# Attention scores of two heads: 128-row products of high and low parts, or 64-row products side by side

## The chip, the core and the metric

The kernel runs on one core of one Trainium2 chip, as one launch. The metric is the device time of a run in microseconds (us). The kernel before takes 1893.79 us, the median of three runs (1891.71 to 1893.83). The profile was taken on one further execution, of 1892.18 us, whose profiled span is 1890.4 us.

The engines are named as in the profile: PE is the matrix engine, PEld its weight loads, DVE the vector engine, ACT the scalar engine, POOL the general one, SP the one that issues most DMAs. PE writes its products to PSUM, which has eight banks of 128 partitions by 512 fp32 numbers.

## The reference

The program is one inference step of a two-layer decoder: a retention layer, a projection to shared keys and values, and a stick-breaking attention layer with 16 heads of 64 numbers each. A prompt of 1024 tokens and eight sample groups of eight tokens use the same weights. The change touches only the attention, where this is computed for each head of the prompt:

```
z = q @ k.T * scale + bias            # (1024 queries x 1024 keys), 64 numbers in each product
mask = k_pos < q_pos                  # strictly causal
log_keep = where(mask, log_sigmoid(-z), 0)
tail_excl = sum of log_keep over the later keys of the same query
w = where(mask, exp(log_sigmoid(z) + tail_excl), 0)
o = w @ v
```

The queries and keys are normed before, and the output is multiplied by a gate.

## The kernel before, in words

**The work.** The function `attention` handles the 16 heads in eight pairs. A pair has eight units, one for each block of 128 queries; unit t needs the (t + 1) * 128 keys up to its own. A unit is cut into pieces. A piece with up to 256 keys holds both heads of the pair next to each other (a joint piece); a wider one, 384 or 512 keys, holds one head, so its two heads are two pieces. Units with more than 512 keys have two such spans. That makes 20 pieces per pair, 160 in all, and with 8 pieces for the samples 168 (`NPC`). Odd pairs go through their units from wide to narrow, even ones from narrow to wide.

**Stages of a piece.** `score` (PE, L1715) writes the scores of a piece to one of the two banks of `z`. `stick` (ACT, L1910) reads them twice, for sigmoid(-z), called `keep`, and sigmoid(z), called `take`. `weigh` (DVE, L2033) makes the running product of `keep` (a scan, L2052) and multiplies it into `take` (L2062). `turn_w` (PE, L1750) transposes the result into one of the two banks of `wt`, ACT (or for a few pieces DVE) copies it to `w_t`, and `attend` (PE, L1761) multiplies the values by it into `out`, which has two banks, one for each group of four units. DVE's `gate` (L2111) empties a bank of `out`.

**Order.** Every engine runs a loop over p, and the order is written out in these loops. In step p PE does `score(p + 1)`, a turn of keys, queries or sample pages if one is due, `turn_w(p - 2)` and `attend(p - 3)`; `attend` has work only where a piece closes a unit's span, that is, for a joint piece or the second head. Between these, in the first part of the section, PE does the projection of the gates (`project`, lines L2934 to L2936, L2956 and L2957), cut into slices that are dealt out over the steps by `slices_before`. ACT does `stick(p)`, the copy of the weights of p - 2 and the copies of what was turned; DVE does `weigh(p - 1)` and the rest. `score(p + 1)` waits until `take` of piece p - 1 is made (L1718), which frees the bank of `z`.

**Precision.** Queries and keys are fp32. A 4-byte operand in the reduced format fp32r goes through PE once, so the kernel works with two parts. A key row is split into a high part (rounded to fp32r, by ACT, L1898) and the rest (DVE, L2025); the two are laid side by side in `k_parts`, 64 + 64 numbers, and turned, so that `k_t` has the high part of the 64 numbers on partitions 0 to 63 and the low part on 64 to 127. The queries of a head are loaded twice side by side (`load_q`, four DMAs, L1326), turned, and the turned 128-row block is kept as `q_hi` (ACT, L1908) and the rest `q_lo` (DVE, L2030). A head's scores are then two accumulated fp32r products of 128 rows each, L1741 with `q_hi` and L1745 with `q_lo`. A joint piece adds the bias by a product (L1744), and the span with the own block adds the mask by a product (L1747). All that is turned for queries, keys and samples goes through one bank, `kq`, and each turn waits until the one before has been copied out (`kq_taken`). Queries are turned in 32 groups of two units (`QG = 2`, four transposes each), keys in four turns of four transposes per pair.

## Time and profile before

| what | value |
|---|---|
| median of the runs | 1893.79 us |
| the profiled execution | 1892.18 us |
| its span | 1890.4 us |
| PE busy | 1808.4 us, 96% |
| DVE busy | 1054.8 us, 56% |
| ACT busy | 810.1 us, 43% |
| PE, DVE, ACT busy from 1366 to 1560 us | 179.53, 156.91, 140.42 us |
| PE, DVE, ACT busy from 1560 to 1781 us | 200.79, 191.27, 179.63 us |

The attention section runs from the first score at 1366.2 us to the last `attend` at 1781 us. The gate projection is dealt out in its first half, the samples in its second. Busy times of PE include the modelled end of each product, so that successive products overlap in time; what a product costs in a stream is the distance from its start to the next start. PE runs at 2.4 GHz for almost the whole program.

One fp32 product (not fp32r) leaves two MATMUL records and two weight loads in the trace.

### The profile page before, as it was taken

What the parts mean: (1) busy time and instruction counts of PE and PEld (TensorE: products, weight loads), DVE (VectorE), ACT (ScalarE), POOL (GpSimd) and SP (SyncE); (2) the same over time, 40 slices, a digit from 0 to 9 for tenths busy, and PEclk for the clock granted to TensorE, in tenths of its full rate; (3) what the DMA queues carried; (4) which work ended last, traced back from release to release, by engine and by line L of the source; (5) the groups of instructions that cost most, each with busy time, mean ns of one, the idle gap of its engine ahead of it and who ended that gap; (6) DMA issues with size and microseconds to landing.
All of it is one profiled execution on the core that took longest, in us unless ns stands there. A gap on an engine that the chain in (4) does not pass through costs nothing. (4 is left out here: it accounts for less than half of the span.)

```text
span 1890.4 us, 28031 instructions
## 1 busy us (share of the span) xinstructions
PE 1808.4 (96%) x10103; PEld 1427.4 (76%) x10103; DVE 1054.8 (56%) x1975; ACT 810.1 (43%) x1682; POOL 81.0 (4%) x140
## 2 busy tenths in 40 slices
PE   5899999999999999999999999999989988999998
PEld 2678787878787878677788777888777766676677
DVE  4553535353535353624546345755178788888852
ACT  3742323232323333412344223533367677878620
POOL 2000000000000000000000000011000000000000
PEclk8899999999999999999999999999999999999999
DMA  9231212131303040583424563223323253553152
GB/s 324 84 93 58 93 57 92 57 99 50 125 23 126 22 148 0 194 272 96 133 62 173 203 214 111 82 92 113 110 59 84 79 164 102 157 154 127 57 178 95
DMA packets 184939, 215.54 MB, mean 114 GB/s; under 512 B 45352, under 2 KB 142560, under 8 KB 183809
## 3 DMA queue, kind: packets, MB, share of 16 engines
q1 hardware_dynamic: 171146, 167.17, 28.9%
q0 software_dynamic: 13696, 47.08, 6.5%
q8 instruction: 60, 0.98, 0.2%
q14 instruction: 37, 0.30, 0.1%
HBM read 165.39 MB, written 48.83 MB: 113 GB/s over the span
## 5 line engine op out<-in xcount | busy, mean ns | idle before, releaser
L475 PE MATMUL rt_acc<-rt_w_hi,rt_h_hi 128*128 128x512 f32 x504 | 203.5, 404 | 1.0 <-DVE rt_h_lo L1014 1.0
L477 PE MATMUL rt_acc<-rt_w_hi,rt_h_lo 128*128 128x512 f32 x504 | 197.4, 392 | 0.0
L476 PE MATMUL rt_acc<-rt_w_lo,rt_h_hi 128*128 128x512 f32 x504 | 196.7, 390 | 0.0
L1057 DVE TENSOR_TENSOR rt_by_cos<-rt_raw,rt_cos 128x256 f32<-128x256 f32 (+1 forms) x72 | 30.5, 424 | 243.9 <-ACT rt_raw L887 243.9
L898 ACT COPY rt_qk_t<-rt_tr 128x256 f32<-128x256 f32 (+1 forms) x72 | 26.0, 361 | 278.6 <-PE rt_tr L706 278.6
L2946 PE MATMUL kq_acc<-kq_w_hi,kq_h 128*128 128x512 f32 x320 | 127.3, 398 | 0.0
L2949 PE MATMUL kq_acc<-kq_w_hi,kq_h 128*128 128x512 f32 x320 | 124.8, 390 | 0.0
L2947 PE MATMUL kq_acc<-kq_w_lo,kq_h 128*128 128x512 f32 x320 | 124.8, 390 | 0.0
L1938 ACT COPY pa_w_t<-pa_wt 128x512 f32<-128x512 f32 (+2 forms) x160 | 86.7, 542 | 72.2 <-PE pa_wt L1756 69.1
L477 PEld LDWEIGHTS rt_acc<-rt_w_hi,rt_h_lo 128*128 128x128 f32 x504 | 94.6, 188 | 20.5
L475 PEld LDWEIGHTS rt_acc<-rt_w_hi,rt_h_hi 128*128 128x128 f32 x504 | 94.9, 188 | 19.1 <-DVE rt_h_lo L1014 1.4
L2052 DVE TENSOR_TENSOR_SCAN pa_after_key<-pa_keep 128x128 f32<-128x128 f32 (+3 forms) x128 | 101.6, 814 | 12.9 <-ACT pa_keep L1919 6.1
L476 PEld LDWEIGHTS rt_acc<-rt_w_lo,rt_h_hi 128*128 128x128 f32 x504 | 95.0, 189 | 17.9 <-issue 0.2
L764 PE MATMUL rt_acc_g<-rt_h_hi,rt_g_hi 128*128 128x512 f32 x256 | 105.8, 413 | 0.0
L2062 DVE TENSOR_TENSOR pa_take<-pa_take,pa_after_key 128x512 f32<-128x512 f32 (+2 forms) x160 | 102.1, 638 | 5.5
L766 PE MATMUL rt_acc_g<-rt_h_lo,rt_g_hi 128*128 128x512 f32 x256 | 100.3, 392 | 0.0
L765 PE MATMUL rt_acc_g<-rt_h_hi,rt_g_lo 128*128 128x512 f32 x256 | 100.1, 391 | 0.0
L1756 PE MATMUL pa_wt<-ident,pa_take 128*128 128x128 f32 x592 | 94.0, 276 | 3.9 <-DVE pa_take L2062 2.2
L1741 PE MATMUL z<-pa_k_t,pa_q_hi 128*128 128x128 f32 (+3 forms) x192 | 79.7, 415 | 17.4 <-DVE pa_q_lo L2030 8.0
L1927 ACT ACTIVATE pa_keep<-z,pa_bias 128x512 f32<-128x512 f32 (+1 forms) x128 | 86.2, 673 | 16.4 <-PE z L1747 7.2
L2052 DVE TENSOR_TENSOR_SCAN pa_after_key<-pa_keep,pa_after_key 128x512 f32<-128x512 f32 x64 | 82.0, 1281 | 6.7 <-ACT pa_keep L1927 2.3
L1928 ACT ACTIVATE pa_take<-z,pa_bias 128x512 f32<-128x512 f32 (+1 forms) x128 | 85.7, 669 | 0.0
(414 smaller groups left out, 4168.7 us busy)
## 6 DMA issues: line engine op xcount, KB each, us to landing
ro_a_raw<-retained SPq DMA_DIRECT2D x14, 1024.0 KB, 5.8
op_ada<-in_ada_w SPq DMA_DIRECT2D x8, 1024.0 KB, 11.4
rt_w_raw<-in_ret_w_in SPq DMA_DIRECT2D x16, 512.0 KB, 5.1
rt_w_raw<-in_ret_w_in SPq DMA_DIRECT2D x8, 1024.0 KB, 7.8
rt_old<-in_state_ret SPq DMA_DIRECT2D x8, 1024.0 KB, 6.0
rt_g_raw<-in_ret_w_in SPq DMA_DIRECT2D x8, 1024.0 KB, 5.2
out_st_sample<-rt_new POOLq DMA_DIRECT2D x8, 1024.0 KB, 8.0
kq_w_raw<-in_sb_w_in SPq DMA_DIRECT2D x4, 2048.0 KB, 9.0
```

Source lines behind the costliest of these rows:

```text
L475: nc.tensor.matmul(dst, h_hi[:, k, cols], w_hi[:, k, :], start=k == 0, stop=False)
L476: nc.tensor.matmul(dst, h_hi[:, k, cols], w_lo[:, k, :], start=False, stop=False)
L477: last = nc.tensor.matmul(dst, h_lo[:, k, cols], w_hi[:, k, :], start=False, stop=k == KD - 1)
L764: nc.tensor.matmul(dst, g_hi[:, k, part], h_hi[:, k, cols], start=k == 0, stop=False)
L765: nc.tensor.matmul(dst, g_lo[:, k, part], h_hi[:, k, cols], start=False, stop=False)
L766: last = nc.tensor.matmul(dst, g_hi[:, k, part], h_lo[:, k, cols], start=False, stop=k == KD - 1)
L1756: last = nc.tensor.transpose(wt[:, p % 2, b * P:(b + 1) * P], take[:, p % TR, b * P:(b + 1) * P], ps.ident[:])
L2052: nc.vector.tensor_tensor_scan(ring[:, c0:c0 + n][:, ::-1], k[:, ::-1], k[:, ::-1], seed, ALU.mult, ALU.bypass).then_inc(scanned, 1)
L2062: nc.vector.tensor_tensor(own, own, later, ALU.mult).then_inc(weighed, 1)
L2946: nc.tensor.matmul(dst, hi, w_hi, start=k == 0, stop=False)
L2947: last = nc.tensor.matmul(dst, hi, w_lo, start=False, stop=t == NPT and k == KD - 1)
L2949: last = nc.tensor.matmul(dst, proj.lo(t)[:, k, :], w_hi, start=False, stop=k == KD - 1)
```

## The change

- `k_parts`, the splits of keys and of queries and their semaphores are gone, on ACT and DVE, in the attention and at the end of the projection before it. `k2` gets two buffers.
- Keys and queries are kept in fp32 as they are turned: 128 numbers of a row are the two heads of a pair, so a turned block has head 0 on partitions 0 to 63 and head 1 on 64 to 127. A pair now has two turns of keys instead of four; queries are turned in 16 groups of four units (`QG = 4`), with one DMA for what were four.
- The scores of two heads are computed together, in a round: two fp32 products of 64 rows, one at row position 0 and one at row position 64, each to a bank of its own. There are two pairs of banks (`z2`), used in turn by rounds. The bias and mask products stay, 128 rows each. A round is two pieces where a piece holds one head, else one. `score` of the next round is issued at the first piece of a round.
- Two banks (`wt`) take all that is turned, weights, keys, queries, new rows and pages, in one alternating sequence, and each turn waits until the turn two before it has been copied out (`wait_bank`). `kq` is gone, and `out` has one bank.
- On DVE the gate of p - 4 is moved ahead of `weigh(p - 1)`.

```diff
@@ attention @@
-        QG = 2
+        QG = 4
+        rounds = []
+        for p in range(NPC):
+            if pieces[p].heads == (1,):
+                rounds[-1].append(p)
+            else:
+                rounds.append([p])
+        round_of = {p: r for r, members in enumerate(rounds) for p in members}
...
-        z, wt, acc, kq, out = held.z, bank("wt", 2), bank("acc"), bank("kq"), bank("out", 2)
+        z2, wt, acc, out = (held.z, bank("z2", 2)), bank("wt", 2), bank("acc"), bank("out")
...
+        turns = [("k", 0, 0), ("q", 0), ("k", 0, 1)]
+        for p in range(NPC):
+            if p in q_slots:
+                turns.append(("q", q_slots[p]))
+            if p in k_slots:
+                turns.append(("k", *k_slots[p]))
...
+            if p >= 2:
+                turns.append(("w", p - 2))
...
+        def wait_bank(engine, *turn):
+
+            n = turn_of[turn] - 2
...
+            if kind == "k":
+                engine.wait_ge(k_taken, 2 * key[0] + key[1] + 1)
+            elif kind == "q":
+                engine.wait_ge(q_taken, key[0] + 1)
...
+            else:
+                wait_taken(engine, key[0])
...
@@ PE @@
-            def score(p):
-                at = pieces[p]
-                if p >= 2:
-                    pe.wait_ge(sticks, p - 1)
+            def score(r):
+                p = rounds[r][0]
+                at, z = pieces[p], scores_of(p)
+                if r >= 2:
+                    pe.wait_ge(sticks, rounds[r - 2][-1] + 1)
...
-                for i, hh in enumerate(at.heads):
-                    dst, keys = z[:, p % 2, i * n:(i + 1) * n], k_t[:, pair % 2, hh, c0:c0 + n]
-                    nc.tensor.matmul(dst, q_hi[:, g % 2, hh, at.u % QG, :], keys, start=True, stop=False)
-                    if len(at.heads) == 2:
+                own, joined = c0 + n == (t + 1) * P, len(at.heads) == 2
+                for hh in range(2):
+                    part = slice(hh * DH, (hh + 1) * DH)
+                    last = nc.tensor.matmul(z[:, hh, 0:n], q_t[part, g % 2, at.u % QG, :], k_t[part, pair % 2, c0:c0 + n],
+                                            start=True, stop=not (own or joined), tile_position=(hh * DH, 0))
...
-            turn_k(0, 0)
-            project(0, 2)
-            turn_k(1, 0)
-            project(2, 4)
+            project(0, 3)
             turn_q(0)
...
             for p in range(NPC):
-                if p + 1 < NPC:
-                    score(p + 1)
+                if p == rounds[round_of[p]][0] and round_of[p] + 1 < len(rounds):
+                    score(round_of[p] + 1)
...
@@ DVE @@
-            rest_q(0)
...
             for p in range(NPC):
+                if p >= 4:
+                    gate_at(p - 4)
                 if p:
                     weigh(p - 1)
                 if p >= 2:
                     take_w(p - 2)
-                if p - 1 in q_slots:
-                    rest_q(q_slots[p - 1])
-                if p >= 4:
-                    gate_at(p - 4)
```

How the change moves instructions shows at three places. The first is PE near the end of the section, in the last pair, where two units of 512-key spans and a narrow one follow each other. Before, `z<-pa_k_t,pa_q_hi` and `z<-pa_k_t,pa_q_lo` are the two products of one head's scores, `pa_wt<-ident` turns weights, `pa_kq<-ident` turns queries:

```order
L1741 MATMUL z<-pa_k_t,pa_q_hi 128x512
L1745 MATMUL z<-pa_k_t,pa_q_lo 128x512
L1747 MATMUL z<-pa_far_r_3481,pa_ident_r_3482 128x128
L1756 MATMUL pa_wt<-ident,pa_take 128x128 x2
L1805 MATMUL pa_acc<-sa_v_pages_8036,pa_w_t 32x256 x8
L1805 MATMUL pa_acc<-sa_new_rows_8035,pa_w_t 32x256 x4
L1741 MATMUL z<-pa_k_t,pa_q_hi 128x512
L1745 MATMUL z<-pa_k_t,pa_q_lo 128x512
L1747 MATMUL z<-pa_far_r_3481,pa_ident_r_3482 128x128
L1676 MATMUL pa_kq<-ident,pa_q4_3487 128x128 x4
L1756 MATMUL pa_wt<-ident,pa_take 128x128 x4
```

The same place of the changed kernel; `pa_q_t` are the turned queries, and "x2" at a score are the products of the two heads:

```order
L1771 MATMUL z<-pa_k_t,pa_q_t 128x512 x2
L1779 MATMUL z<-pa_far_r_3481,pa_ident_r_3482 128x128 x2
L1788 MATMUL pa_wt<-ident,pa_take 128x128 x2
L1790 MATMUL pa_wt<-ident,pa_take 64x128
L1816 MATMUL pa_out<-pa_w_t,pa_v2 64x128 x8
L1788 MATMUL pa_wt<-ident,pa_take 128x128 x2
L1837 MATMUL pa_acc<-sa_v_pages_8024,pa_w_t 32x256 x8
L1837 MATMUL pa_acc<-sa_new_rows_8023,pa_w_t 32x256 x4
L1771 MATMUL pa_z2<-pa_k_t,pa_q_t 128x384 x2
```

The scores of both heads stand together, the next step begins without any, and the turn of queries at this place is gone. The second place is DVE at the start of the section, before; `pa_after_key<-pa_keep` is the scan, `pa_q_lo` the rest of the queries, `pa_k_parts` that of the keys:

```order
L2030 TENSOR_TENSOR pa_q_lo<-pa_kq,pa_q_hi 128x512
L2140 TENSOR_TENSOR pa_g_out_3478<-pa_acc,pa_g_out_3478 128x512
L2052 SCALAR_TENSOR_TENSOR pa_after_key<-pa_keep 128x128 x2
L2062 TENSOR_TENSOR pa_take<-pa_take,pa_after_key 128x256
L2030 TENSOR_TENSOR pa_q_lo<-pa_kq,pa_q_hi 128x512
L2052 SCALAR_TENSOR_TENSOR pa_after_key<-pa_keep 128x256 x2
L2062 TENSOR_TENSOR pa_take<-pa_take,pa_after_key 128x512
L2052 SCALAR_TENSOR_TENSOR pa_after_key<-pa_keep 128x384
L2062 TENSOR_TENSOR pa_take<-pa_take,pa_after_key 128x384
L2030 TENSOR_TENSOR pa_q_lo<-pa_kq,pa_q_hi 128x512
```

The same place of the changed kernel:

```order
L2148 TENSOR_TENSOR pa_g_out_3478<-pa_acc,pa_g_out_3478 128x512
L2060 SCALAR_TENSOR_TENSOR pa_after_key<-pa_keep 128x128 x2
L2070 TENSOR_TENSOR pa_take<-pa_take,pa_after_key 128x256
L2060 SCALAR_TENSOR_TENSOR pa_after_key<-pa_keep 128x256 x2
L2070 TENSOR_TENSOR pa_take<-pa_take,pa_after_key 128x512
L2060 SCALAR_TENSOR_TENSOR pa_after_key<-pa_keep 128x384
```

The three `pa_q_lo` instructions are gone, and scans and multiplications follow each other without them. The third place is PE a little earlier, from the second score of the program on; first before:

```order
L1688 MATMUL pa_kq<-ident,pa_k_parts_3477 128x128 x4
L1741 MATMUL z<-pa_k_t,pa_q_hi 128x256
L1744 MATMUL z<-pa_bias_parts_3485,pa_share_3486 128x256
L1745 MATMUL z<-pa_k_t,pa_q_lo 128x256
L1747 MATMUL z<-pa_far_r_3481,pa_ident_r_3482 128x128
L1741 MATMUL z<-pa_k_t,pa_q_hi 128x256
L1744 MATMUL z<-pa_bias_parts_3485,pa_share_3486 128x256
L1745 MATMUL z<-pa_k_t,pa_q_lo 128x256
L1747 MATMUL z<-pa_far_r_3481,pa_ident_r_3482 128x128
L1676 MATMUL pa_kq<-ident,pa_q4_3487 128x128 x4
```

And in the changed kernel:

```order
L1771 MATMUL pa_z2<-pa_k_t,pa_q_t 128x256 x2
L1776 MATMUL pa_z2<-pa_bias_parts_3485,pa_share_3486 128x256
L1779 MATMUL pa_z2<-pa_far_r_3481,pa_ident_r_3482 128x128
L1776 MATMUL pa_z2<-pa_bias_parts_3485,pa_share_3486 128x256
L1779 MATMUL pa_z2<-pa_far_r_3481,pa_ident_r_3482 128x128
L1708 MATMUL pa_wt<-ident,pa_q4_3487 128x128 x4
L1771 MATMUL z<-pa_k_t,pa_q_t 128x384 x2
```

The turn of keys ahead of this score is gone, and the score of the third unit (384 keys) uses queries that were turned with the first two.

## Rows read from the trace of the kernel before

**Rows 1.** Busy us of each engine in the attention's two halves.

```profile
1366.00:1560.00 194.00, 179.53 (x1363) 141.95 (x1361) 156.91 (x207) 140.42 (x265) 8.52 (x13) 0.98 0.36 101
1560.00:1781.00 221.00, 200.79 (x1899) 152.09 (x1897) 191.27 (x280) 179.63 (x362) 2.14 (x4) 1.00 0.43 127
```

**Rows 2.** DVE and ACT groups by form, 1366 to 1781 us: count, busy, mean ns, idle before.

```profile
L2052 DVE TENSOR_TENSOR_SCAN pa_after_key<-pa_keep,pa_after_key 128x512 f32<-128x512 f32 x64 | 82.0, 1281 | 6.7 <-ACT pa_keep L1927 2.3 <-DVE pa_g_t L2118 0.6
L2062 DVE TENSOR_TENSOR pa_take<-pa_take,pa_after_key 128x512 f32<-128x512 f32 x112 | 77.5, 692 | 3.9
L2030 DVE TENSOR_TENSOR pa_q_lo<-pa_kq,pa_q_hi 128x512 fp32r<-128x512 f32 x31 | 21.3, 686 | 7.0 <-ACT pa_q_hi L1908 7.0
L2025 DVE TENSOR_TENSOR pa_k_parts<-pa_k,pa_k_parts 128x512 fp32r<-128x512 f32 x14 | 9.6, 687 | 0.7
L1908 ACT CAST pa_q_hi<-pa_kq 128x512 fp32r<-128x512 f32 x31 | 18.4, 594 | 0.8 <-PE pa_kq L1676 0.8
```

**Rows 3.** Waits of PE, 1366 to 1781 us: total us, times, longest.

```profile
PE z L1741 <- DVE pa_q_lo L2030: 8.0, 5, 3.9
PE pa_kq L1688 <- ACT pa_k_t L1902: 3.1, 9, 0.8
```

**Rows 4.** Timeline of PE, 1764 to 1769 us: start, length, line, tiles, shapes.

```profile
1766.74 0.50 PE L1741 MATMUL z<-pa_k_t,pa_q_hi 128*128 128x512 f32 x1
1767.08 0.40 PE L1745 MATMUL z<-pa_k_t,pa_q_lo 128*128 128x512 f32 x1
1767.32 0.22 PE L1747 MATMUL z<-pa_far_r,pa_ident_r 128*128 128x128 f32 x1
1767.38 0.60 PE L1676 MATMUL pa_kq<-ident,pa_q 128*128 128x128 f32 x4
1767.81 0.60 PE L1756 MATMUL pa_wt<-ident,pa_take 128*128 128x128 f32 x4
1768.34 0.44 PE L1784 MATMUL pa_out<-pa_w_t,pa_v 128*64 128x128 f32 x4
1768.71 0.44 PE L1741 MATMUL z<-pa_k_t,pa_q_hi 128*128 128x384 f32 x1
1768.99 0.34 PE L1745 MATMUL z<-pa_k_t,pa_q_lo 128*128 128x384 f32 x1
```

**Rows 5.** Timeline of PE, 1366 to 1379 us.

```profile
1368.92 0.36 PE L1741 MATMUL z<-pa_k_t,pa_q_hi 128*128 128x256 f32 x1
1369.12 0.27 PE L1744 MATMUL z<-pa_bias_parts,pa_share 128*128 128x256 f32 x1
1369.23 0.28 PE L1745 MATMUL z<-pa_k_t,pa_q_lo 128*128 128x256 f32 x1
1369.35 0.22 PE L1747 MATMUL z<-pa_far_r,pa_ident_r 128*128 128x128 f32 x1
...
1369.87 0.63 PE L1676 MATMUL pa_kq<-ident,pa_q 128*128 128x128 f32 x4
1374.38 0.66 PE L1741 MATMUL z<-pa_k_t,pa_q_hi 128*128 128x384 f32 x1 [3.88 <-DVE pa_q_lo L2030]
```

**Rows 6.** Timeline of PE in the retention layer, 127.4 to 128.8 us.

```profile
127.48 0.48 PE L745 MATMUL rt_acc<-rt_v,rt_k_own 32*128 32x256 f32 x1
...
127.50 0.48 PE L745 MATMUL rt_tr<-rt_v,rt_k_own 32*128 32x256 f32 x1
127.80 0.37 PE L745 MATMUL rt_acc<-rt_v,rt_k_own 32*128 32x256 f32 x1
...
128.02 0.38 PE L745 MATMUL rt_acc<-rt_v,rt_k_own 32*128 32x256 f32 x1
```

**Rows 7.** Timeline of PE, 1763 to 1800 us: fp32 products of 128 rows.

```profile
1781.41 6.28 PE L1880 MATMUL z<-ao_w_raw,ao_a_raw 128*128 128x512 f32 x14
```

**Rows 8.** Timeline of DVE, 1366 to 1379 us.

```profile
1371.84 0.69 DVE L2140 TENSOR_TENSOR pa_g_out<-pa_acc,pa_g_out 128x512 f32<-128x512 f32 x1 [6.10 <-ACT pa_g_out L1972]
...
1373.56 0.68 DVE L2030 TENSOR_TENSOR pa_q_lo<-pa_kq,pa_q_hi 128x512 fp32r<-128x512 f32 x1
```

More of the change, by code:

```diff
@@ L1322, in load_q @@
         rows_of = ps.q_rows[0:SEQ, :].rearrange("(t p) c -> p t c", p=P)
-        src = rows_of[:, 4 * half:4 * half + 4, pair * 2 * DH:(pair + 1) * 2 * DH].rearrange("p t (h d) -> p t h d", h=2)
-        for a in range(2):
-            for hh in range(2):
-                sp.dma_start(self.q4[:, m % 3, :, hh, a, :], src[:, :, hh, :]).then_inc(loaded, 16)
+        src = rows_of[:, 4 * half:4 * half + 4, pair * 2 * DH:(pair + 1) * 2 * DH]
+        sp.dma_start(self.q4[:, m % 3], src).then_inc(loaded, 16)
 class Held:
@@ L1518, in wait_taken, with turn_bank, scores_of @@
                 engine.wait_ge(w_taken_a, len([n for n in range(p + 1) if not on_vector(n)]))
+        turns = [("k", 0, 0), ("q", 0), ("k", 0, 1)]
[4 more added lines that the diff above has]
+                turns.append(("k", *k_slots[p]))
+            if p in new_slots:
+                turns.append(("new", new_slots[p]))
+            if p in page_slots:
+                turns.append(("pages", *page_slots[p]))
+            if p >= 2:
+                turns.append(("w", p - 2))
+        turns += [("w", NPC - 2), ("w", NPC - 1)]
+        turn_of = {turn: n for n, turn in enumerate(turns)}
+        def turn_bank(*turn):
+            return wt[:, turn_of[turn] % 2, :]
+        def wait_bank(engine, *turn):
+            n = turn_of[turn] - 2
+            if n < 0:
+                return
+            kind, key = turns[n][0], turns[n][1:]
+            if kind == "k":
+                engine.wait_ge(k_taken, 2 * key[0] + key[1] + 1)
+            elif kind == "q":
+                engine.wait_ge(q_taken, key[0] + 1)
+            elif kind == "new":
+                engine.wait_ge(*((new_taken, key[0] + 1) if key[0] < 2 else (sa_ready, 1)))
+            elif kind == "pages":
+                engine.wait_ge(sk_taken, 4 * key[0] + key[1] + 1)
+            else:
+                wait_taken(engine, key[0])
+        def scores_of(p):
+            return z2[round_of[p] % 2]
         def sample_before(p, lag):
@@ L1879, in _ @@
                 a = held.raw[:, 0, k, :] if k < held.LOADED else held.own_raw[:, t * P:(t + 1) * P]
-                nc.tensor.matmul(z[:, 0, :], a, first.raw[:, k, :], start=k == 0, stop=k == KD - 1).then_inc(first_made, 1)
+                nc.tensor.matmul(held.z[:, 0, :], a, first.raw[:, k, :], start=k == 0, stop=k == KD - 1).then_inc(first_made, 1)
             t += 1
@@ L1906, in take_q @@
                 if g >= 2:
[L1907 to L1908 removed]
+                    act.wait_ge(scored, round_of[ends[QG * (g - 1) - 1]] + 1)
+                nc.scalar.copy(q_t[:, g % 2].rearrange("p n c -> p (n c)"), turn_bank("q", g)).then_inc(q_taken, 1)
             def stick(p):
[L1911 to L1912 removed]
+                at, n, z = pieces[p], pieces[p].wide, scores_of(p)
+                act.wait_ge(scored, round_of[p] + 1)
                 if p >= 2:
@@ L2720, in _ @@
                     nc.scalar.copy(pairs.ident_r[:], ps.ident[:])
-                    act.wait_ge(k_loaded, 16)
-                    for hh in range(2):
-                        nc.scalar.copy(pairs.k_parts[:, hh, :, 0, :], by_head(pairs.k2, hh)).then_inc(k_hi_s, 1)
         @block.vector
```

196 lines of the change are left out of this document (77 added, 119 removed).

## The prediction

> **What bounds the kernel now.** I read the busy times by stage first. The change touches only the attention, 1366 to 1781 us. In its first half PE is busy 179.53 of 194 us and DVE 156.91; in the second PE 200.79 of 221, DVE 191.27, ACT 179.63 [rows 1]. So the first half, with the gate projection in it, is PE's. In the second PE and DVE are nearly level: where pieces of 512 keys follow each other, DVE needs 1281 + 692 ns, 1.97 us, for each, and splits of queries and keys on top [rows 2]; where there are narrow pieces and sample pages, PE has more to do. Next the waits: PE's longest single wait is one of 3.9 us for the low part of the queries, and all five waits of that kind are 8.0 us; waits for the one bank of turned keys come to 3.1 us, and sample turns add some more [rows 3]. Last the timelines, which give what a product costs from start to start.
>
> The whole section is one chain of three engines in step, so a microsecond saved counts only on the engine that is late there. I count by halves.
>
> **Turns.** Queries go from 32 groups to 16 of four transposes, keys from 32 turns to 16. That is 128 transposes less. Four take 1767.38 to 1767.81, 0.43 us [rows 4], so 0.108 us each, 13.8 us on PE, about half of it in each half of the section.
>
> **The score products.** Before, a head at 512 keys costs 0.34 + 0.24 = 0.58 us (1766.74, 1767.08, 1767.32), at 384 keys 0.28 us and then, between the 0.24 and the 0.12 of its neighbours, 0.18 us, together 0.46 [rows 4]. At 256 keys it is 0.20 + 0.12 us (the bias product between them stays) for the first head [rows 5], and about 0.29 for the second, which follows a product and not a turn; at 128 keys some 0.25 per head, since no product there starts less than 0.11 us after another. A pair has six rounds at 512 keys and two each at 384, 256 and 128: 6 x 1.16 + 2 x 0.92 + 2 x 0.61 + 2 x 0.50 = 11.0 us, times eight pairs 88 us.
>
> After, an fp32 product is two records. At 128 rows the trace has 14 records of 512 columns, each 0.59 us long, in 6.28 us, so (6.28 - 0.59) / 13 = 0.44 us from start to start [rows 7]; a product is 0.88 us. Two heads one after the other would be 1.76 us and lose against 1.16. It hangs on whether products at different rows of the array run at the same time. The retention layer has the case, with four strips of 32 rows in four banks: four records start between 127.48 and 127.50, the next four from 127.80, the next from 128.02, each 256 columns wide [rows 6]. They run together, at 0.22 us for 256 columns, the price of one, and the first step to the second record is 0.10 us longer. I take the same for two strips of 64 rows. A round is then 0.43 + 0.43 + 0.10 = 0.96 us at 512, 0.74 at 384, 0.53 at 256, 0.31 at 128 (columns in proportion). Per pair: 6 x 0.96 + 2 x 0.74 + 2 x 0.53 + 2 x 0.31 = 8.9 us, times eight 71 us. That is 17 us less.
>
> Against it: PE must change over between full products and strips. The last of four turns of weights starts at 1767.81 + 0.60 - 0.28 = 1768.13, would end its turn at 1768.24, and the first `attend` product, in strips of 64 columns, starts at 1768.34 [rows 4]: 0.10 us. Each of the 96 prompt rounds is now followed by full products, a change-over that was not there. Ahead of a score one is new only where no `attend` stands before it: counted in the order, 43 of the rounds. 139 times 0.10 is 13.9 us. So the scores give 17 - 14 = 3 us; bounds: 17 with free change-overs, -11 if one costs 0.20.
>
> The Trainium skill ("TensorEngine Tiling (Array Packing)", Key Properties) speaks against the change here: "Changing tiling mode (not just tile) drains the TensorE". It names no price; by it every change-over counts, and the 0.10 us of the row bears it out. Without it the sum would be 14 us lower.
>
> **Start of the section.** PE sits idle 3.88 us until 1374.38 because the score of unit 2 needs the low part of its queries, and that DVE instruction (1373.56) stands behind a gate product, which itself waited 6.10 us, and the first `weigh` [rows 5, 8]. Now unit 2's queries were turned with the first two units', the score is done in that gap, and PE goes on when the first weights are ready, about 1373.6. I count 1.5 us, and 0.5 for less time at the lower clock after it: 2 us.
>
> **What leaves DVE and ACT.** DVE loses 31 query splits at 0.686 and 14 key splits at 0.687 us, 31 us [rows 2]; half of it, 15.5 us, in the second half. ACT loses 16 query copies at 0.594 us [rows 2], as many key copies and 14 key splits, some 28 us. In the first half PE hides all of it: nothing. In the second, where DVE is late it counts fully, where PE is late it does not. Bounds 0 and 15.5. PE's own saving there is 7 us of turns, and the four later waits for query parts go, 8.0 - 3.9 = 4.1 us [rows 3]. So the half is shorter by 11 us where PE is late and by 15.5 where DVE is; I take 11 in all, since nothing says which.
>
> **What the change adds in waits.** (1) A piece's weights now share two banks with keys, queries and pages. After such a turn in step p, `turn_w` of step p + 1 waits for ACT's copy of it; `attend` and the next scores stand behind it on PE, and ACT's copy of the weights behind these. There are 15 query, 14 key, 3 new-row and 32 page turns, 64. The copy is 0.59 us and stands behind ACT's `stick` and weight copy, while PE has a score (0.96) or an `attend` in between. Bounds 0 and 0.6 us each, 0 to 38 us; nearest row: the nine waits of key turns for ACT's copy in the old single bank, 3.1 us together, 0.35 each [rows 3]. PE had slack in part of these: I take 0.05 each, 3 us, net of the old waits that go. (2) `out` has one bank: 15 times `attend` waits for DVE's gate, one 0.69 us product like the one in rows 8, while PE turns weights for 0.43 us. 0.1 us each, 1.5 us; bounds 0 and 0.7 each, 10. (3) Scores come in lumps: a step with 0.96 us of scores, then one with none. ACT's copy waits up to 0.4 us in the first, PE in the second; the scores are ready a step earlier, so ACT no longer waits for them. I call it even; bounds -4 and +8.
>
> The DMAs for queries become one of 512-byte rows instead of four; nothing waits for them in the rows, so 0. The splits before the section run beside PE's projection: 0.
>
> **Sum.** First half: turns -7, scores -1.5, start -2, new waits +1.5: -9. Second half: -11 with its turns, scores -1.5, new waits +3: -9.5. Together -18.5, in round figures -19, against the execution of 1892.18 us: 1873. The median of the runs stands 1.6 us above that execution; that is less than this sum can tell, so it stays at 1873.
>
> **Rivals.** (A) Deeper gain: DVE was what held PE up in all of the second half, its 15.5 us come in full, and PE's idle time, 14.5 and 20.2 us in the two halves [rows 1], shrinks by 5 us. For it: DVE's 191 us is as high as PE's real load, since PE's busy time includes modelled ends. Against it: ACT waits for turned weights, so PE is late often. Then -15.5 - 9 - 5 = -30: 1862. (B) Little gain: change-overs to strips of rows cost 0.15 us and not 0.10 (+7), and narrow pieces and sample pages hold PE so that of the second half's 11 us only the 5 us that follow wide pieces come (+6): -19 + 7 + 6 = -6, 1886. For it: PE's load there is the highest of the three [rows 1]; against it: the first record's extra 0.10 us is counted already [rows 6]. (C) Slower: the shared turn banks. If the wait behind each of the 64 turns is over 0.33 us, the gain is gone; at the 0.6 us of a whole copy it is 38 us against the 3 counted, 1873 + 35 = 1908; at 0.45 us, which I take for it, 1873 + 26 = 1899. For it: PE and ACT are then in lock-step, and a `turn_w` held up holds the score of the next round. Against it: PE has 0.43 to 1.5 us of other work between, and ACT runs ahead on `stick`. (D) The strips do not run together, and the change does not do what it says. For it nothing in the rows, only that 64-row strips and this pairing don't occur. Then 48 x 0.86 + 16 x (0.64 + 0.43 + 0.21) = 62 us more: 1936.
>
> **Chances.** Forecast 0.47 (1867 to 1882), A 0.25, B 0.12, C 0.12, D 0.04. A difference under 0.2%, 3.8 us, can't be told from none. Faster than 1890: forecast, A and most of B, 0.82; within: 0.05 from B and the edge of C; slower 0.13. The range: A down to 1855 and B in full, 1892; C and D and the deepest of A are left out.
>
> **What would show it.** In the profile after: the score records of two heads start within 0.02 us of each other and the next two 0.53 us later at 512 columns (strips run together); the first mask product starts about 0.10 us after their end (change-over); 64 + 64 transposes of queries and keys at 0.108 us; no wait of 3.9 us at the start; DVE's busy time in the section lower by 31 us; waits of `turn_w` for ACT's copies of keys, queries or pages under 5 us in total. Score starts 0.43 us apart one by one would make it wrong at once (D), and large waits of turned weights for ACT copies would (C).

## The result, and the profile after

The changed kernel takes 1899.14 us (median, 1896.48 to 1901.40), the kernel before 1891.89 us (1890.73 to 1893.83, now six runs) on the same chip. The ratio is 1.0041, 95% interval 1.0030 to 1.0051: some 8 us slower, where 1873 and 19 us less were forecast. Of the rivals, C had named 1899, but for a reason that explains only part of it, as will be seen.

Busy time of each engine in the two halves, as in [rows 1] (the second half now goes on past 1781 us; the product behind the last `attend` starts at 1787.4):

```profile
1366.00:1560.00 194.00, 178.51 (x1290) 116.90 (x1289) 145.28 (x185) 126.90 (x239) 8.52 (x13) 0.99 0.27 86
1560.00:1781.00 221.00, 200.40 (x1791) 130.54 (x1792) 174.87 (x250) 167.26 (x333) 2.15 (x4) 0.98 0.38 120
```

PE's busy times are those of [rows 1] to about 1 us, while DVE has 28 us less to do and ACT 26. The work did leave DVE and ACT; the section got longer all the same. The groups by form (1366 to 1788 us) that answer to [rows 2]:

```profile
L2060 DVE TENSOR_TENSOR_SCAN pa_after_key<-pa_keep,pa_after_key 128x512 f32<-128x512 f32 x64 | 82.0, 1281 | 12.7 <-ACT pa_keep L1949 8.4 <-DVE pa_g_t L2126 0.9
L2070 DVE TENSOR_TENSOR pa_take<-pa_take,pa_after_key 128x512 f32<-128x512 f32 x112 | 77.5, 692 | 3.9
L2126 DVE TENSOR_TENSOR pa_g_t<-pa_out,pa_g_t 128x512 f32<-128x512 f32 x14 | 9.7, 691 | 21.7 <-PE pa_out L1816 21.7
L1929 ACT COPY pa_q_t<-pa_wt 128x512 f32<-128x512 f32 x15 | 8.9, 590 | 2.1 <-PE pa_wt L1708 2.1
```

The scan and the weighing cost what they did. Queries are now 15 copies on ACT and nothing on DVE. New is DVE's idle time of 21.7 us ahead of the gate product. Next the waits from 1366 to 1790 us, as in [rows 3]:

```profile
DVE pa_g_t L2126 <- PE pa_out L1816: 21.7, 13, 2.4
PEld pa_wt L1788 <- DVE pa_take L2070: 21.4, 26, 1.6
...
DVE pa_after_key L2060 <- ACT pa_keep L1949: 16.8, 23, 1.6
...
PE pa_wt L1788 <- DVE pa_take L2070: 8.9, 13, 1.3
...
PE pa_wt L1741 <- ACT sa_k_t L1983: 5.8, 6, 1.3
```

The waits for the low part of the queries (8.0 us) are gone. In their place DVE waits for PE's sums at the gate, and PE waits for DVE's weights before it turns them. A circle of two engines that wait for each other has no idle engine to relieve.

A round of two heads at 512 keys and what follows it, against [rows 4] (timeline of PE, 1766 to 1769.2 us):

```profile
1766.98 0.65 PE L1788 MATMUL pa_wt<-ident,pa_take 128*128 128x128 f32 x4
1767.56 1.13 PE L1771 MATMUL z<-pa_k_t,pa_q_t 64*128 64x512 f32 x4
1768.62 0.44 PE L1779 MATMUL z<-pa_far_r,pa_ident_r 128*128 128x128 f32 x2
1768.90 0.41 PE L1788 MATMUL pa_wt<-ident,pa_take 128*128 128x128 f32 x2
```

And the same view from 1767.8 to 1768.3 us, which cuts the group of four and shows only the two later records:

```profile
1768.10 0.60 PE L1771 MATMUL z<-pa_k_t,pa_q_t 64*128 64x512 f32 x2
```

Both heads' second records stand in one row of 0.60 us, the length of one record: the strips run together, 0.54 us behind the first two. Four transposes between two groups of strips take 0.58 us (1766.98 to 1767.56), where four among full products take 0.43 [rows 4]: 0.09 more from the last transpose to the first strip, and 0.05 more from the first transpose, which stands behind strips, to the second. From the second records to the first mask product it is 0.52 us, 0.43 for the 512 columns and 0.09 for the change back. Then comes what I had not counted: two mask products take 0.28 us (1768.62 to 1768.90), and a mask product alone 0.06 in [rows 4]. Without strips ahead the same two take 0.17 us (second experiment below). So the first product after the change back holds up the second by another 0.10 us; the other 0.05 us beyond twice 0.06 comes with the new order, in which two masks stand one behind the other.

The start, against [rows 5]:

```profile
1371.69 1.13 PE L1771 MATMUL pa_z<-pa_k_t,pa_q_t 64*128 64x512 f32 x4 [1.02 <-ACT pa_take L1942]
...
1374.76 0.66 PE L1788 MATMUL pa_wt<-ident,pa_take 128*128 128x128 f32 x4 [1.32 <-DVE pa_take L2070]
```

The stall of 3.88 us is gone, and two of 1.02 and 1.32 us stand in its place: 1.5 us less, as forecast. DVE's first gate product comes at 1370.80 after 10.46 us of waiting, against 1371.84 and 6.10 us in [rows 8]; no query split stands behind it:

```profile
1370.80 0.69 DVE L2148 TENSOR_TENSOR pa_g_out<-pa_acc,pa_g_out 128x512 f32<-128x512 f32 x1 [10.46 <-ACT pa_g_out L1996]
1371.41 0.73 DVE L2060 TENSOR_TENSOR_SCAN pa_after_key<-pa_keep 128x128 f32<-128x128 f32 x2
```

**PE's section added up.** I gave each PE record of the section the time to the next record's start, and split off idle time (a wait) and the 0.10 us at each change between full products and strips. The section here begins with the first turn of keys (1360.1 us before, 1358.1 after) and ends with the product behind the last `attend` (1781.4 and 1787.4), so it takes in some projection ahead of the first score. In us:

| | before | after | change |
|---|---|---|---|
| score products | 82.7 | 72.0 | -10.7 |
| turns of queries and keys | 28.4 | 15.2 | -13.2 |
| changes between full and strips (218, 369) | 21.8 | 37.9 | +16.1 |
| mask, bias, weight turns (they stand behind the changes) | 80.7 | 93.1 | +12.4 |
| all else | 162.4 | 163.6 | +1.2 |
| waits | 45.4 | 47.4 | +2.0 |
| section | 421.3 | 429.3 | +8 |

PE's own time was to fall by 17 us (turns 14, scores 3); it rose by 5.8. The 37.9 us are 1 us more than 369 times 0.10, so the +16.1 of the changes is 15 to 16. (The counts are those of the traces; a count of the order, in the expectation of the fifth experiment, gives 217 and 376.)

The rows of the changes and of what stands behind them grow by 28.5 us, 0.19 for each of 151 more changes. Not all of this is the price of a change. A second count, which takes a product's usual step from the trace itself and draws the line between work and wait a little otherwise, gives 79.0 us before and 92.4 after for masks, biases and weight turns, and 85.5 for the second experiment below, which has the new frame and no strips. So about half of the 12.4 us comes with the order of the new frame. What is left is 15 to 16 and some 7 us, 0.15 us for a change.

**The clock.** The two profiled executions differ in it as well. In this section PE's granted clock was at its lower level, 1.2 GHz, for 17.0 us after the change, in four stretches, of which these are two (stretch and length, busy us of PE, PEld, DVE, ACT and POOL, then the granted clock as a share of 2.4 GHz):

```profile
1358.50:1361.90 3.40, 3.40 (x11) 2.72 (x9) 1.78 (x1) 0.59 (x1) 0.00 (x0) 0.50 0.66 190
...
1559.90:1566.70 6.80, 6.69 (x34) 4.88 (x34) 5.27 (x12) 2.40 (x4) 0.00 (x0) 0.50 0.14 42
```

Before the change it was one stretch of 6.8 us:

```profile
1373.00:1379.80 6.80, 5.42 (x23) 4.76 (x23) 5.86 (x10) 3.21 (x7) 0.37 (x1) 0.50 0.40 93
```

They stand at or just behind idle time of PE: 2.39 us until 1358.10, 1.74 us until 1560.01, and before the change the 3.88 us of [rows 5]. In the first of them projection products start 0.43 us apart, behind it 0.23. PE was busy for 16.5 us of the four stretches and for 5.4 us of the one before; at half speed that costs at most 8.3 and 2.7 us. So up to 5.6 us of the 5.8 by which PE's own time rose in these two executions go with the clock. Over all runs it is less: the mean granted clock is 0.988 in the six runs of the changed kernel and 0.990 in the 78 runs of the kernel before that stand beside the experiments, and of these the ones at 0.988 took 1894.5 us and the ones at 0.991 1891.0, 1.2 us for 0.001. By that, an estimate, some 2 us of the 8 go with the clock. Whether more waits brought the lower clock or it came otherwise, no run tells.

### The profile page after: what moved, and what is told of

Its sections match the earlier page's. It is cut to its first block and busy times, and to the rows that moved or that the text cites. A ratio compares the mean times of both kernels' runs of the same rounds, so it can differ in the third digit from the quotient of the medians.

```text
span 1896.1 us, 27547 instructions
## 1 busy us (share of the span) xinstructions
PE 1812.8 (96%) x9975; PEld 1385.2 (73%) x9975; DVE 1029.3 (54%) x1927; ACT 787.7 (42%) x1634; POOL 81.2 (4%) x140
## 5 line engine op out<-in xcount | busy, mean ns | idle before, releaser
L1788 PEld LDWEIGHTS pa_wt<-ident,pa_take 128*128 128x128 f32 x592 | 67.2, 142 | 40.7 <-DVE pa_take L2070 21.4
L1816 PE MATMUL pa_out<-pa_w_t,pa_v 128*64 128x128 f32 x1152 | 85.5, 285 | 1.0 <-ACT pa_w_t L1961 0.7
L2382 DVE TENSOR_TENSOR ro_a_lo<-ro_a_raw,ro_a_hi 128x1024 fp32r<-128x1024 f32 x28 | 33.0, 1221 | 90.1 <-ACT ro_a_hi L2341 90.1
```

Of the source, the lines that this page charges most:

```text
L1788: last = nc.tensor.transpose(dst[:, b * P:(b + 1) * P], take[:, p % TR, b * P:(b + 1) * P], ps.ident[:])
```

## The experiments

Each was run beside the kernel before; ratios are against it, with 95% intervals. 0.1% is 1.9 us. The clock bears on some of them: the two with the longest waits have the lowest mean, 0.979 and 0.986. The expectations speak of three theories. Theory 1: PE's own time, above all the changes between full products and strips, ate the gain. Theory 2: the lumps of scores did. Theory 3: the frame did, that is the shared turn banks, the one output bank and the gate's place.

**Scores of the next round issued later** (changed kernel, one line):

```
-                if p == rounds[round_of[p]][0] and round_of[p] + 1 < len(rounds):
+                if p == rounds[round_of[p]][-1] and round_of[p] + 1 < len(rounds):
                     score(round_of[p] + 1)
```

> The changed kernel with one edit: the scores of the next round are issued at the last piece of a round, not at its first. In rounds of two pieces they then stand right behind an `attend`, so that 43 change-overs between full products and strips go, and the step that had no scores gets them. Theory 1 (PE's own time, above all 0.20 us for each change-over, 0.10 before the first strip or full product and 0.10 for the weights of the one behind it, has eaten the saving): 43 x 0.20 = 8.6 us less, 1890 to 1891. Theory 2 (the lumps of scores hold up the turns of weights, whose waits went from 4.7 to 19.1 us): the waits of turned weights fall back under 8 us as well, 1880 to 1885. Theory 3 (the shared turn banks cost the waits): the waits stay, 1890.

Measured 1888.74 us, 0.9982 (0.9973 to 0.9991): 0.59% less than the changed kernel. The waits of the section fall from 47.4 to 39.6 us, and its changes from 369 to 353, 16 and not the 43 expected. The place of the scores, which I had called even, costs some 10 us in this frame. By what mechanism is not shown: the waits of turned weights did not fall under 8 us, as theory 2 had it (21.4 before, 24.0 now for the wait of PEld on DVE's `take`), and the time lies between the two theories.

**Full products in place of strips** (changed kernel; each head's scores are two products of 128 rows in the rounded form, which add both heads up and use no low part):

```
-                    last = nc.tensor.matmul(z[:, hh, 0:n], q_t[part, g % 2, at.u % QG, :], k_t[part, pair % 2, c0:c0 + n],
-                                            start=True, stop=not (own or joined), tile_position=(hh * DH, 0))
+                    for time in range(2):
+                        last = nc.tensor.matmul(z[:, hh, 0:n], q_t[:, g % 2, at.u % QG, :], k_t[:, pair % 2, c0:c0 + n],
+                                                start=time == 0, stop=time == 1 and not (own or joined))
```

> The changed kernel without strips: each head's scores are two products of 128 rows in the reduced format on the turned block as it is, instead of one fp32 product of 64 rows. It leaves out that the two heads are kept apart (both heads get the sum over 128 rows) and the low parts. Rounds, banks, turns and waits are those of the changed kernel. Theory 1: some 150 change-overs at 0.20 us go, 30 us, and the products cost 83 us as in the kernel before and not 72, 11 us more: 19 us less than the changed kernel, 1880. Theories 2 and 3 (lumps or shared banks hold it): PE only waits longer, 1893 to 1899.

Measured 1886.09 us, 0.9971 (0.9962 to 0.9980), so the strips cost 0.70%, 13 us. PE's own time is 362.5 us against 381.8 in the changed kernel: of 19.3 us, 13 reach the end. That is between what theory 1 (1880) and the other two (1893 to 1899) expected. Two masks behind full products, to be set against 0.28 us behind strips:

```profile
1754.46 0.34 PE L1779 MATMUL z<-pa_far_r,pa_ident_r 128*128 128x128 f32 x2
1754.63 0.40 PE L1788 MATMUL pa_wt<-ident,pa_take 128*128 128x128 f32 x2
```

They take 0.17 us. 151 changes at 0.15 us are 23 us, the shorter score records give some 4 back, and 19 are left, as measured; some of it can be the clock, since PE was busy at the lower one for 6.7 us here and for 16.5 in the changed kernel.

**No splits on DVE** (kernel before; the queries' low parts are zero and the keys' are those of the first pair):

```
-                if p - 1 in q_slots:
-                    rest_q(q_slots[p - 1])
...
-                if p - 1 in k_split_slots:
-                    split_k(k_split_slots[p - 1])
```

> The kernel before with the splits of queries and keys taken from DVE: the low parts of the queries are zero, set once, those of the keys stay those of the first pair. PE and ACT do the same work. It measures the term of the prediction for DVE's relief alone. The prediction's reckoning: 11 us in the second half less the 4 us of waits that are counted in it, and the start, so 9 to 13 us less, 1879 to 1883. Theory 1 (PE's own time bounds both halves): only the waits for low parts, 8.0 us, go, and in part come back elsewhere: 3 to 6 us less, 1886 to 1889.

Measured 1883.72 us, 0.9961 (0.9948 to 0.9973): DVE's relief by itself is worth 8 us, all of it in PE's waits (45.4 to 36.4). It lies between the prediction's reckoning (9 to 13) and theory 1 (3 to 6).

**Half the turns** (kernel before; 118 transposes fewer, half of each turned block stale):

```
-                for hh in range(2):
+                for hh in range(2 if g < 1 else 1):
...
-                for n in range(4):
+                for n in range(4 if head < 2 else 2):
```

> The kernel before with half of the transposes in each turn of queries and keys after the first (118 transposes less); the other half of the turned block stays what was in the bank. ACT and DVE copy as much as before. It measures the prediction's term for turns alone. If PE bounds the section: 118 x 0.108 = 12.7 us less, 1879. If PE is late in only half of it: 6 us less, 1886. If ACT and DVE bound it: nothing, 1892.

Measured 1885.38 us, 0.9966 (0.9953 to 0.9979). The transposes cost what was forecast, 12.5 us of PE's own time; 6.5 reach the end, as if PE were late in half of the section, and PE's waits grow by 4.

**Strip work put together** (the version with late scores, and PE's last projection and fold of a step ahead of `attend`):

```
+                project(slices_before(p, 2), slices_before(p + 1, 0))
                 if p >= 3:
                     attend(p - 3)
-                project(slices_before(p, 2), slices_before(p + 1, 0))
```

> The changed kernel with the late scores of the experiment before, and in each step the last slices of the gate projection and the folds of the samples ahead of `attend`, so that `attend` and the scores of the next step stand together as strips. The order counts 376 change-overs in the changed kernel, 361 with late scores and 353 here (217 in the kernel before). Theory 1: 8 x 0.20 = 1.6 us less than with late scores, 1887. If `attend` is later than its copy for other reasons: up to 2 us more, 1889 to 1891.

Measured 1888.50 us, 0.9981 (0.9971 to 0.9990), the same as without. It saved 8 changes only, so it says nothing for or against theory 1.

**Shared turn banks alone** (kernel before; queries, keys and sample turns go to the weights' two banks):

```
-                pe.wait_ge(*kq_taken[0])
+                wait_bank(pe, "q", g)
...
-                        last = nc.tensor.transpose(kq[:, 0, at:at + P], src, ps.ident[:])
+                        last = nc.tensor.transpose(turn_bank("q", g)[:, at:at + P], src, ps.ident[:])
```

> The kernel before with the two turn banks shared by weights, keys, queries, new rows and pages, in one alternating sequence, as the changed kernel has them; the bank of its own for keys and queries is unused. Nothing else is changed. It measures the shared banks alone. Theory 3 (the shared banks cost the waits of turned weights, 4.7 to 19.1 us in the changed kernel): 8 to 14 us more, 1900 to 1906. Theories 1 and 2: -1 to +3 us, 1891 to 1895. The prediction counted 3 us for it.

Measured 1916.33 us, 1.0127 (1.0112 to 1.0142): 24 us more, where I had counted 3, and more than any theory expected. Its waits, 1366 to 1790 us, name the place:

```profile
PEld pa_wt L1786 <- DVE pa_take L2092: 26.1, 16, 3.2
PE pa_wt L1786 <- DVE pa_q_lo L2060: 24.4, 19, 3.0
```

The turn of weights waits, 19 times at 1.3 us, for the low part of the queries that lie in the bank, a split that DVE reaches a step later.

**The changed kernel's frame with the arithmetic of before** (rounds of scores, four score banks, shared turn banks, one output bank; high and low parts as before). Its core against the changed kernel:

```
-        k_t = sb("k_t", [P, 2, SEQ])
-        q_t = sb("q_t", [P, 2, QG, P])
+        k_t = sb("k_t", [P, 2, 2, SEQ], F32R)
+        q_hi = sb("q_hi", [P, 2, 2, QG, P], F32R)
+        q_lo = sb("q_lo", [P, 2, 2, QG, P], F32R)
```

> The changed kernel's frame with the arithmetic of the kernel before: scores of both heads in one lump at the first piece of a round, four score banks, shared turn banks, one bank of `out`, the gate ahead of `weigh`; but high and low parts, 128-row products, 32 groups of queries and 32 turns of keys as before, and all splits. It adds no change-overs. Theory 1 (the change-overs are the loss): the frame is free, 1890 to 1894. Theory 2 (lumps and the rest of the frame): 7 to 12 us more than before, 1899 to 1904.

Measured 1946.45 us, 1.0283 (1.0269 to 1.0296). With the old arithmetic the frame costs 54 us, where the dearest expectation was 12; the new arithmetic wins 46 of them back. The granted clock averages 0.979 here against 0.990, so by the 1.2 us above some 13 of the 54 go with it. Its waits from 1366 to 1790 us are those of the changed kernel, and the low part's besides:

```profile
PEld pa_wt L1800 <- DVE pa_take L2107: 36.0, 20, 4.0
PE pa_wt L1800 <- DVE pa_q_lo L2075: 33.5, 18, 3.7
DVE pa_g_t L2163 <- PE pa_out L1828: 28.4, 13, 4.2
```

**One output bank, and the gate ahead of `weigh`** (kernel before; the edits that make `out` one bank are left out below):

```
+                if p >= 4:
+                    gate_at(p - 4)
                 if p:
                     weigh(p - 1)
...
-                if p >= 4:
-                    gate_at(p - 4)
```

> The kernel before with one bank of `out` and the gate ahead of `weigh`, as in the changed kernel; nothing else. The prediction counted 1.5 us for the 15 waits. All theories: 0 to 3 us more, 1892 to 1895; if DVE's gate, now ahead of the scan of the next piece and waiting for `attend`, holds DVE up, 4 to 8 us more.

Measured 1898.42 us, 1.0035 (1.0022 to 1.0048). That is the case in which the gate holds DVE up (4 to 8 us more). The wait that it makes, from 1366 to 1790 us:

```profile
DVE pa_g_t L2118 <- PE pa_out L1784: 11.2, 12, 1.4
```

**The gate behind the weighing** (changed kernel; the edit is the last one turned round, between `weigh` and `take_w`):

```
-                if p >= 4:
-                    gate_at(p - 4)
                 if p:
                     weigh(p - 1)
+                if p >= 4:
+                    gate_at(p - 4)
```

> The kernel after the change (1899.1 us, 1.0041 of before) with one edit: VectorE gates the finished output of a group of four tiles behind the weighing of the same step and no longer ahead of it. It still has one output bank. Theory 3 (the frame of shared banks and waits costs the gain; in the kernel after, the gate waits 21.7 us for the sums of four steps ago, 13 times 2.4 us, and the scan and the weights queue behind it): the chain of scans keeps running, so 5 to 10 us less than after, 1889 to 1894, and 'gate waits for sums' falls under 8 us. Theory 1 (PE's own time of change-overs sets the end): PE's busy time is the same and so is the span, within 2 us of 1899. Against theory 3: with one output bank PE then waits for the gate before its next sums, 16 times up to 1.3 us, which could give most of it back.

Measured 1894.62 us, 1.0014 (1.0004 to 1.0024), 0.27% less than the changed kernel, at the edge of theory 3. The gate's wait for the sums (it was 21.7 us, 13 times up to 2.4 us, so 1.7 on average and not the 2.4 of the expectation) is down to 0.7 us, the scan waits longer for `keep` instead (16.8 to 27.7 us), and PE's wait before `attend` grows from 1.5 to 4.4 us, the price of the one bank itself (1.5 forecast).

**Urgent turn first** (changed kernel; queries, keys and pages are turned behind the weights):

```
                 project(slices_before(p, 0), slices_before(p, 1))
                 if p >= 2:
                     turn_w(p - 2)
+                if p in q_slots:
+                    turn_q(q_slots[p])
+                if p in k_slots:
+                    turn_k(*k_slots[p])
...
```

> The kernel after the change with one edit: in a step of PE the turn of queries, keys and sample pages comes behind the turn of the weights and no longer ahead of it, and the two shared turn banks are handed round in that order. Nothing is left out. Theory 3: the next turn of weights then waits for the copy of weights that the scalar engine makes first, and the turn after it for the copy of queries or keys, a step more of slack; the waits of the turn of weights fall from 19 us to 12 or less and the time by 4 to 8 us, to 1891 to 1895. Theory 1: same PE work, same time within 2 us of 1899.

Measured 1886.37 us, 0.9974 (0.9963 to 0.9985): 0.67%, 13 us less, more than expected. The waits that vanish are not those of the weights' turns (19.1 before, 22.8 now) but those of the turns moved: sample pages 8.7, keys 4.3 and queries 1.1 us become 0.4 together. My reason was wrong in its detail: what had stood in the way was the other turn's own wait for a bank, with the weights queued behind it.

**All three together**:

> The kernel after the change with three edits: the scores of the next round are issued at the last piece of the round and not at the first (alone 10.4 us less than after), the gate behind the weighing, and the turns of queries and keys behind the turn of weights. If the waits are separate stalls (theory 3), their gains add up and it takes 1875 to 1883, less than before's 1892 by 9 us or more. If PE's change-overs are a floor (theory 1: 382 us of products and change-overs in the section against 376 before), it stays near 1888.

Measured 1877.53 us, 0.9919 (0.9906 to 0.9932), faster than both kernels. The three gains were 0.59, 0.27 and 0.67%, in sum 1.53; together they bring 1.22. That is what separate stalls were expected to give (1875 to 1883), and not the floor of 1888. Its waits from 1366 to 1790 us:

```profile
ACT pa_w_t L1961 <- PE pa_wt L1788: 76.8, 80, 2.5
...
PEld pa_wt L1788 <- DVE pa_take L2070: 27.4, 34, 2.1
...
PE pa_wt L1788 <- DVE pa_take L2070: 10.4, 11, 2.0
```

What is left is the chain of a piece itself: DVE weighs, PE turns, ACT copies.

**All three, with full products in place of strips** (the edit of the second experiment on top):

> The kernel with all three reorderings (0.9919 of before, 1877.5 us), and in place of the two strips of 64 rows in full precision per pair of heads, two products of 128 rows in the rounded form for each head. What it computes changes: both heads are added into the same scores and no low part is multiplied in. It takes away about 140 change-overs between the two forms. Theory 1 (change-overs cost PE 0.20 us each): PE's products and change-overs in the section fall by 140 x 0.10 of change-over and some 3 us of products, and since the waits are now fewer, most of it shows: 1860 to 1867. Theory 3 (waits alone set the end): within 3 us of 1877.

Measured 1867.67 us, 0.9874 (0.9858 to 0.9889), 0.45% less than with strips. 136 changes fewer and 15.8 us less of PE's own time give 10 us; the changes go on costing once the waits are few. That is just above what theory 1 expected (1860 to 1867): again only half to two thirds reach the end.

**Shared turn banks alone, turns behind the weights** (the sixth and the tenth edit on the kernel before):

> The kernel before with its turns of queries, keys and sample pages in the two banks of the weights (alone +24 us, 1916.3), and those turns placed behind the turn of the weights in each step. All that is computed is as before. If the place in the order is what makes the shared banks dear, more than half of the 24 us comes back: 1896 to 1903. If it is the number of banks (61 copies of queries and keys and their low parts now stand in the same two banks), it stays at 1910 or above.

Measured 1882.12 us, 0.9945 (0.9931 to 0.9959): 34 us less than with the old order, and less than either expectation (1896 to 1903, or above 1910). The wait that was 24.4 us is no longer among the longer ones, from 1366 to 1790 us:

```profile
PEld pa_wt L1786 <- DVE pa_take L2092: 14.3, 23, 1.1
...
PE z L1771 <- DVE pa_q_lo L2060: 7.1, 4, 3.9
```

**Turns behind the weights alone** (kernel before, its own turn bank kept):

> The kernel before with one edit: in each step of PE the turn of queries, keys and sample pages comes behind the turn of the weights; the turns keep their own bank. All is computed as before. If the order is a gain of its own (the weights, on which the sums wait, are no longer queued behind a turn that is not urgent), 1879 to 1884, as with shared banks (1882). If it is only a repair of the shared banks' wait, it stays within 3 us of 1891.8.

Measured 1879.12 us, 0.9937 (0.9924 to 0.9949). So the order is a gain of its own, 0.63% here and 0.67% in the changed kernel, and does not explain why that one is slower. It does set the price of shared banks: 24 us in the old order, and in this one 3 us by the medians (1882.12 to 1879.12) or 0.08% by the ratios, which is within their intervals and can't be told from nothing.

```profile
1366.00:1560.00 194.00, 181.12 (x1380) 143.24 (x1379) 160.20 (x217) 141.89 (x268) 8.52 (x13) 0.98 0.36 102
1560.00:1781.00 221.00, 210.56 (x1910) 159.13 (x1910) 195.64 (x285) 182.11 (x368) 2.14 (x4) 0.99 0.42 124
```

In these busy times by halves PE reaches 210.56 us in the second half against 200.79 in [rows 1], with the same work: the section ends at 1767.4 us, and the product behind it already runs in the rest.

**The frame with the arithmetic of before, all three reorderings**:

> The changed kernel's frame (rounds of scores in four banks, two shared turn banks, one output bank) with the kernel before's high and low parts (1946.4 us) and the three reorderings. If the frame's 54 us are its avoidable waits, it falls by more than the 22 us that they take off the changed kernel, to 1900 or below; if they are the price of the banks that are missing, to 1915 to 1925.

Measured 1886.19 us, 0.9968 (0.9957 to 0.9979). The reorderings take 60 us off it, so the 54 us were waits that could be avoided. Of the frame's 54 us some 6 are left (0.9968 against 0.9937), and the new arithmetic is then worth 0.49%, 9 us (0.9968 to 0.9919).

## Why the prediction was wrong

The changed kernel's +0.41% can be laid out in four parts, three of them measured and the frame as what remains. Half the turns -0.34%, no splits on DVE -0.39%; from their sum, 0.9927, to the frame with that arithmetic and full products, 0.9971: +0.44%; strips +0.70%. (That the first two add up was not run, ACT's relief is contained in the frame's part, and so is what goes with the lower clock.) In us, beside the forecast:

| part | forecast | measured |
|---|---|---|
| turns | -14 | -6.4 |
| DVE and ACT relieved, start | -6 | -7.4 |
| frame: banks, gate, lumps (the remainder) | +4.5 | +8.3 |
| scores: strips against full products | -3 | +13.2 |
| sum | -19 | +8 |

- **The scores, the step that failed most.** "139 times 0.10 is 13.9 us." The count was low (151 in the trace), and 0.10 us is two thirds of the price: it is what stands ahead of a change, as [rows 4] show, and another 0.05 us (turns) to 0.10 us (masks) sits behind it, before the second product; 0.15 us in all, on average. 151 times that is 23 us for 13.9. The row from which I read the 0.10 gives only the start of the first product behind a change, not that of the second. Changes and what stands behind them grow by 28.5 us, against 10.7 won by shorter records; that is a loss of 17.8 us on PE, outside of the bound that I wrote (-11, at 0.20 us a change). Some 6 us of it come from the new order of the products and not from the changes; the sum had no term for them. That the two strips run together, at 0.54 us for the first records and 0.43 + 0.09 for the next, was right, and 72.0 us of score products against 71 forecast too; the old ones took 82.7 and not 88, which is 5 us of the error. Rival B had this mechanism at 0.15 us, on 139 changes.
- **The turns.** The size on PE was right, 13.2 us for 13.8. "A microsecond saved counts only on the engine that is late there" was written down and then not applied: all 13.8 were counted. Half the turns alone bring 6.5 of 12.5; fewer strips bring 13 of 19 and 10 of 16. In this section half to two thirds of a PE microsecond reach the end, the rest turns into waits for DVE and ACT.
- **The relief of DVE.** Right in size when it stands alone (8 us). In the changed kernel it does not show in PE's waits (45.4 and 47.4 us). DVE's wait at the gate is at most a part of the reason: with the wait gone (the gate behind the weighing) 5 us come back.
- **The new waits.** For the shared banks "I take 0.05 each, 3 us", though the nearest row had 0.35 us each [rows 3]: 64 times that is 22, and alone in the kernel before they cost 24. The 3 us would do for another order, in which the urgent turn goes first (1882 against 1879, not clear of noise). That PE has "other work between" overlooked that this work stands behind the waiting turn in PE's own queue. The one output bank: 1.5 us forecast, 6 measured with the gate ahead of the weighing; taking that place back in the changed kernel gives 5. The gate's new place was in the change and I gave it no price at all. "I call it even" for the lumps: 10 us.
- **Rival C** named the time but not the cause. In the changed kernel hardly any wait is for ACT's copy of queries or keys by the weights' turn; there are no low parts to wait for, and the frame as a whole costs 8 us and not 26.
- **The signs that I named came true, nearly all, and the time did not.** The strips ran together, the first mask came 0.09 us behind their end, the stall of 3.9 us was gone, DVE had 28 us less to do, and the turn of weights waited 0.9 us for an ACT copy of queries. None of them looked at the second product behind a change, at the waits of the other turns, or at the gate.

What stays open: how the frame's 8 us divide in the changed kernel, since its three reorderings win 23 us and so more than the frame costs; they mend an order that the kernel before had too. And what the 0.05 to 0.10 us behind a change is: no run isolates it. Nor does any run hold the clock fixed.

## What to carry to other kernels

Price a change between full products and strips at both ends, 0.15 us in all here (0.09 ahead of it and 0.05 to 0.10 behind), and count it for the products that follow too. Where three engines work in step as here, take half to two thirds of what the busiest one saves, and give every moved instruction, the gate here, a price in the queue in which it now waits. Before sharing a bank, look at what is queued behind the turn that would wait for it; put the turn on which the chain hangs first.

## What the runs showed of the hardware

- Fp32 products of 64 rows at two places of the array run side by side: both heads' second records of 512 columns stand in one row of 0.60 us. The page of the Trainium skill on tiling, "TensorEngine Tiling (Array Packing)", says under Key Properties that a change of mode drains the engine; the trace agrees (0.58 us against 0.43 for four turns that stand between strips), and shows as well a cost of 0.10 us before the second product behind it (0.28 us for two masks behind strips against 0.17 behind full products).
- Two kernels whose PE busy time differs by less than 0.6% in each half (179.53 and 200.79 us before, 178.51 and 200.40 after) end 6 us apart in the section: busy time of a full engine says that it is full, and not with what.
